# Two convolution modules: the chunk of transform tables moved ahead of the last chunk of input weights, with the second section's transform

## The reference, cut to what matters

```python
def conv_module(h, w_in, b_in, dw_w, dw_b, ln_g, ln_b, w_out):
    a, gt = jnp.split(h @ w_in + b_in, 2, axis=-1)   # (256, 1024) -> two of (256, 1024)
    u = a * jax.nn.sigmoid(gt)
    u = dwconv(u, dw_w, dw_b)                        # depthwise along the tokens, 31 taps
    u = layernorm(u, ln_g, ln_b)
    return jax.nn.silu(u) @ w_out                    # (256, 1024)
```

## Time and profile before

| | us |
|---|---|
| median of three runs | 1610.09 |
| lowest and highest | 1609.86, 1610.27 |
| the profiled execution's own time | 1610.04 |
| span of the profiled execution | 1608.1 |
| TensorE busy in the span | 1573.2 |
| VectorE busy | 1248.2 |
| ScalarE busy | 996.0 |

### The profile page before, as it was taken

How to read it: one execution, slowest core, us unless ns; L and a number is a source line. 1 busy time by engine, 2 the same in 40 slices (tenths; PEclk the granted TensorE clock), 3 DMA queues, 4 the chain that set the end, 5 groups by cost and what they waited for, 6 DMA issues and landing times.

```text
span 1608.1 us, 25361 instructions
## 1 busy us (share of the span) xinstructions
PE 1573.2 (98%) x8810; PEld 1344.2 (84%) x8810; DVE 1248.2 (78%) x1828; ACT 996.0 (62%) x1406; POOL 102.4 (6%) x110
## 2 busy tenths in 40 slices
PE   9999999999999999999999999999999999999998
PEld 9887888878878889868888898868788887878887
DVE  6756888878798887866888886456788887878887
ACT  6576665675676656666666655444666666666664
POOL 0031000000000001340000042000100000000000
PEclk9999999999999999999999999999999999999999
DMA  9434455543645554443555555524555554345553
GB/s 344 153 111 171 181 188 203 183 174 115 239 162 186 195 192 158 165 151 131 183 201 184 189 190 191 195 105 158 183 195 183 185 180 183 140 149 186 185 198 135
DMA packets 43393, 285.44 MB, mean 177 GB/s; under 512 B 5280, under 2 KB 5408, under 8 KB 10688
## 3 DMA queue, kind: packets, MB, share of 16 engines
q1 hardware_dynamic: 40592, 274.96, 47.7%
q0 software_dynamic: 2736, 9.60, 1.8%
HBM read 282.43 MB, written 1.05 MB: 176 GB/s over the span
## 4 chain that ended last, share of the span: by engine, by line
PE 80%; DVE 12%; ACT 5%; issue 3%; DMA 0%; SPq 0%; POOL 0%; DVEq 0%
PE bank L2263 21%; PE bank L2266 10%; PE bank L2162 7%; PE bank L2163 7%; PE bank L2164 7%; PE bank L2112 4%; PE bank L2113 4%; PE bank L2114 4%; DVE w_lo L1230 3%; PE bank L2059 3%; PE bank L2060 3%; PE bank L2061 3%; DVE arena L1527 2%; DVE arena L1513 1%; DVE arena L1510 1%
## 5 line engine op out<-in xcount | busy, mean ns | idle before, releaser
L2263 PE MATMUL bank<-h_both,w_hi 128*128 128x512 f32 x1760 | 554.7, 396 | 10.3 <-DVE arena L1510 6.2
L2266 PEld LDWEIGHTS bank<-h_both,w_lo 128*128 128x128 f32 x1760 | 330.6, 188 | 77.6
L1230 DVE TENSOR_TENSOR w_lo<-raw,w_hi 128x2048 fp32r<-128x2048 f32 (+3 forms) x133 | 289.9, 2180 | 104.3 <-ACT w_hi L698 103.6
L2266 PE MATMUL bank<-h_both,w_lo 128*128 128x256 f32 x1760 | 346.0, 278 | 0.0
L698 ACT ACTIVATE w_hi<-raw 128x2048 fp32r<-128x2048 f32 (+3 forms) x135 | 245.1, 1816 | 100.6 <-PE bank L2164 37.3
L2263 PEld LDWEIGHTS bank<-h_both,w_hi 128*128 128x128 f32 x1760 | 271.6, 189 | 17.6 <-issue 8.2
L1547 DVE TENSOR_TENSOR w_lo<-raw,w_hi 128x2048 fp32r<-128x2048 f32 x120 | 274.1, 2284 | 0.0
L2162 PE MATMUL bank<-w_hi,h_both 128*128 128x512 f32 x632 | 247.9, 392 | 4.2 <-DVE h_both L1541 4.2
L2163 PE MATMUL bank<-w_lo,h_both 128*128 128x512 f32 x632 | 246.2, 390 | 0.0
L2164 PE MATMUL bank<-w_hi,h_both 128*128 128x512 f32 x632 | 246.1, 389 | 0.0
L919 ACT ACTIVATE w_hi<-raw 128x2048 fp32r<-128x2048 f32 x120 | 228.4, 1904 | 0.0
(11 more groups left out here) (236 smaller groups left out, 1858.0 us busy)
## 6 DMA issues: line engine op xcount, KB each, us to landing
raw<-wstream SPq DMA_DIRECT2D x252, 1024.0 KB, 4.8
raw<-wstream SPq DMA_DIRECT2D x8, 256.0 KB, 3.9
raw<-wstream SPq DMA_DIRECT2D x4, 512.0 KB, 8.1
arena<-dilated_bias POOLq DMA_DIRECT2D x8, 256.0 KB, 4.8
arena<-conv_rows POOLq DMA_DIRECT2D x2, 1024.0 KB, 4.7
arena<-window_bias POOLq DMA_DIRECT2D x4, 512.0 KB, 6.0
raw<-wstream SPq DMA_DIRECT2D x4, 384.0 KB, 3.5
cst<-consts SPq DMA_DIRECT2D x1, 1088.0 KB, 11.9
```

The costliest lines, as they stand in the source:

```text
L1230: nc.vector.tensor_tensor(w_lo[:, s, 0:w], raw[:, s, 0:w], w_hi[:, s, 0:w].bitcast(F32), ALU.subtract)\
L2263: nc.tensor.matmul(halves(up_banks(a)[:, m, :]), w[m][0], h_both[:, kt, :, :], start=kt == 0, stop=kt == 7, skip_group_check=True)
L2266: last = nc.tensor.matmul(up_banks(a)[:, m, 0:S], w[m][1], h_hi[:, kt, :], start=False, stop=kt == 7, skip_group_check=True)
```

## The change

The table chunk and the last input chunk change places in the stream: the tables are c8, the last input chunk is c9. On TensorE `transform(1)` stands ahead of `w_in(7)`, and `inverse(0)` is cut into its two token halves, with `transform(2)` between them. On VectorE `wave_parts(0)` goes behind the split of c9, `products(1)` goes ahead of `biased_pair(3, 0)` and `wave_parts(1)` between the two halves of that pair. On ScalarE `wave_parts(1)` goes ahead of the gates of group 3, and the high half of c11 moves from behind `y_evac_conv(0)` to the SiLU loop, behind its second tile. The last input chunk counts on a semaphore of its own (`last_in`), since the tables, which have the lower number, are in use for longer; the end of `inverse(2)` counts both chunks. The third part of section 1 goes to slot 14 of `h_both` in place of slot 4, which `w_in(7)` still reads. The diff, cut to its core:

```diff
-        return [CH] * 5 + [DFT] + [CH] * 3 + [2 * DFT] + [CH] * 4
+        return [CH] * 5 + [DFT] + [CH] * 2 + [2 * DFT] + [CH] * 5
...
+            second = (2, 3, 14)[b]
+            return (slice(8 + 2 * b, 10 + 2 * b), slice(second, second + 1), slice(5 + b, 6 + b))[e]
...
                     def y_evac_conv(e):
                         first, n = section(e)
-                        if e < 2:
-                            act.wait_ge(unwaved, 2 * (k["conv"] - 1) + e + 1)
-                        else:
+                        if e == 1:
+                            act.wait_ge(unwaved, e0 + 3)
+                        elif e == 2:
                             act.wait_ge(first_unwaved, k["conv"])
                         for t in range(1 + (e < 2)):
+                            if e == 0:
+                                act.wait_ge(unwaved, e0 + t + 1)
...
                     split_hi(c0 + 10)
+                    wave_parts(1)
                     gate(3, 0)
                     gate(3, 1)
                     parts(3)
-                    wave_parts(1)
                     y_evac_conv(0)
-                    split_hi(c0 + 11)
                     wave_parts(2)
...
-                        if t == 5:
+                        if t == 1:
+                            split_hi(c0 + 11)
+                        elif t == 5:
                             split_hi(c0 + 12)
...
                     split_lo(c0 + 8)
-                    wave_parts(0)
                     gated_parts(2)
                     split_lo(c0 + 9)
-                    rest_rows(c0 + 9)
+                    wave_parts(0)
+                    rest_rows(c0 + 8)
+                    products(1)
                     biased_pair(3, 0)
+                    wave_parts(1)
                     biased_pair(3, 1)
                     gated_parts(3)
-                    products(1)
-                    wave_parts(1)
                     stats(0, (0,))
                     products(2)
                     wave_parts(2)
...
-                        last.then_inc(unwaved if e < 2 else chunk_used, 1)
+                        if e < 2:
+                            last.then_inc(unwaved, 1)
+                        else:
+                            last.then_inc(chunk_used, 2)
...
-                    w_in(7, 8)
-                    transform(1, c0 + 9)
-                    inverse(0, c0 + 9)
-                    transform(2, c0 + 9)
-                    inverse(1, c0 + 9)
+                    transform(1, c0 + 8)
+                    w_in(7, 9)
+                    inverse(0, c0 + 8, (0,))
+                    transform(2, c0 + 8)
+                    inverse(0, c0 + 8, (1,))
+                    inverse(1, c0 + 8)
                     keep_busy(20, bank[5])
-                    inverse(2, c0 + 9)
+                    inverse(2, c0 + 8)
```

More of the change, by code:

```diff
@@ L307, in build_program @@
         rest_table = sem("rest_table")
+        last_in = sem("last_in")
         unwaved, y_out, y_stats, y_normal = sem("unwaved"), sem("y_out"), sem("y_stats"), sem("y_normal")
@@ L371, in wave_slots @@
         def wave_slots(e, b):
-            return (slice(8 + 2 * b, 10 + 2 * b), slice(2 + b, 3 + b), slice(5 + b, 6 + b))[e]
+            second = (2, 3, 14)[b]
+            return (slice(8 + 2 * b, 10 + 2 * b), slice(second, second + 1), slice(5 + b, 6 + b))[e]
         def glu_slot(g, t):
@@ L1084, in y_evac_conv @@
                         first, n = section(e)
-                        if e < 2:
-                            act.wait_ge(unwaved, 2 * (k["conv"] - 1) + e + 1)
-                        else:
+                        if e == 1:
+                            act.wait_ge(unwaved, e0 + 3)
+                        elif e == 2:
                             act.wait_ge(first_unwaved, k["conv"])
                         for t in range(1 + (e < 2)):
+                            if e == 0:
+                                act.wait_ge(unwaved, e0 + t + 1)
                             ins = nc.scalar.activation(y_conv[:, t, first:first + n], y_bank_conv(e, t)[:, 0:n], ACT.Copy)
-                        ins.then_inc(y_out, 1)
+                            if e == 0:
+                                ins.then_inc(y_out, 1)
+                        if e:
+                            ins.then_inc(y_out, 1)
                     def y_evac_last():
@@ L1726, in biased_pair @@
                             dve.wait_ge(wide_half, k["wide"])
+                        elif g == 3:
+                            dve.wait_ge(last_in, k["conv"])
                         else:
-                            dve.wait_ge(chunk_used, c0 + (1, 3, 6, 8)[g] + 1)
+                            dve.wait_ge(chunk_used, c0 + (1, 3, 6)[g] + 1)
                         if g:
@@ L1798, in stats @@
                         first, n = section(e)
-                        dve.wait_ge(y_out, e0 + e + 1)
                         for t in halves_:
+                            dve.wait_ge(y_out, 4 * (k["conv"] - 1) + (e + 2 if e else t + 1))
                             for at in range(first, first + n, GROUP):
@@ L2097, in feature_chunk, with token_chunk @@
                 last.then_inc(chunk_used, 1)
-            def token_chunk(c, second, h0=0, n_k=4, free=None, wait_h=None, banks=None):
+            def token_chunk(c, second, h0=0, n_k=4, free=None, wait_h=None, banks=None, done=None):
                 pe.wait_ge(lo_done, c + 1)
@@ L2116, in token_chunk @@
                         last.then_inc(wide_half, 1)
-                last.then_inc(chunk_used, 1)
+                last.then_inc(chunk_used if done is None else done, 1)
             def sums(sources, matrix=None, width=S, start=True, stop=True):
@@ L2380, in transform, with inverse @@
                         last.then_inc(waved if e else chunk_used, 1)
-                    def inverse(e, c):
+                    def inverse(e, c, halves_=(0, 1)):
                         _, n = section(e)
@@ L2386, in inverse @@
                         if e == 2:
-                            pe.wait_ge(y_out, e0 + 1)
+                            pe.wait_ge(y_out, 4 * (k["conv"] - 1) + 2)
                         pe.wait_ge(rest_table, k["conv"])
-                        for t in range(2):
+                        for t in halves_:
                             for b in range(2):
@@ L2401, in w_in @@
                         token_chunk(c0 + c, n % 2, free=free, wait_h=k["hlo"] if g == 0 else None,
-                                    banks=(glu_bank(g, 0), glu_bank(g, 1)))
+                                    banks=(glu_bank(g, 0), glu_bank(g, 1)), done=last_in if n == 7 else None)
                     pe.wait_ge(conv_loaded, 112 * k["conv"])
@@ L2691, in pack_weights @@
             ins = [half for flat in pairs for half in (flat[:, :4], flat[:, 4:])]
-            for blocks in (*[[i] for i in ins[:5]], [fwd], *[[i] for i in ins[5:]], [fwd, inv]):
+            for blocks in (*[[i] for i in ins[:5]], [fwd], *[[i] for i in ins[5:7]], [fwd, inv], [ins[7]]):
                 put(*blocks)
```

## The result

The changed kernel took 1615.24 us in the median of 11 runs (1612.68 to 1617.05), the kernel before 1610.4 in 11 runs beside it (1609.86 to 1612.56). The ratio is 1.0026, with a 95% interval of 1.0017 to 1.0036: slower by 4.2 us by the ratio (2.7 to 5.8 us). That is more than the 3.2 us that I called noise, though the lower end of the interval lies within it. The median is 0.2 us above the upper end of the range I gave; the time by the ratio, 1614.3 us, is inside it.

What follows compares the result with a forecast made beforehand. VectorE's backlog was taken as the limit before `inverse(2)`; 1.0 us more in each of two convolutions takes the span from 1608.1 to 1610.1, the execution to 1612.0, the median to 1612.1 us. Range 1609.0 to 1615.0.

Steps and rivals of the forecast that it cites:

- What bounds the kernel: Before `inverse(2)` of each convolution: VectorE's backlog is the limit; at best the 1.13 us TensorE wait goes.
- VectorE's walk: Step-by-step VectorE times from `biased_pair(2, 0)` at 374.70 to group 3's low halves at 391.0 and 391.6.
- The new wait: TensorE, before `transform(2)`: waits 2.2 us for the first low half of group 3, due at 391.0.
- What ends last: Before `inverse(2)`: the 20 transposes end last, so it starts at 398.7 against 397.68, each convolution 1.0 us longer.
- The other edits: c11's high half in the SiLU loop, in time by 0.7 us, and the semaphore, slot and double count: costed at nothing.
- The clock: Rival: TensorE's clock falls behind the wait before `transform(2)`; 1615.9 us with one convolution hit, 1619.7 with both; chance 0.13.
- my bound of 1.5: Upper bound per convolution, if VectorE's two group 3 waits for ScalarE and the first matmul after idling each cost 0.2 more.
- One of my own signs of being wrong: Signs listed: granted clock under 1.00 around 391 us, no wait before `transform(2)`, or a wait before c11's output products.
- The price I set, 3.8 us a fall: `transform(2)` and the second half of `inverse(0)` at half speed: 3.8 us more, between nothing and 7.7 us.
- c11 coming late: Rival: in the SiLU loop c11 is late by up to 1 us in each stage, 1614.1 us; chance 0.04.
- a mild fall of the clock: Allowance in the range's upper part, which reaches to 1615.0 us, for TensorE's clock falling mildly.
- The rival that group 3's low halves would be ready when TensorE asks for them: At 388.8, before `transform(2)`: only TensorE's queue counts, up to 1.3 us gained per convolution, 1607.5 us; chance 0.07.

Runs made afterwards that it cites:

- The experiment with eight transposes: The changed kernel with 8 instead of 20 transposes in front of `inverse(2)`: median 1613.35 us, ratio 1.0017.
- the long execution: Longest of 8 runs of the changed kernel repeated without edit, profiled: 1617.10 us, clock 0.996; the 8 runs had median 1615.74 us, ratio 1.0031.

## Why the prediction was right and wrong

**What bounds the kernel: right.** VectorE's backlog set the start of `inverse(2)` before, and TensorE's own work did not move.

**VectorE's walk: right.** I had group 3's first low half at 391.0 and the second at 391.6; TensorE started at 391.26 and the pair ended at 390.70 + 0.99 = 391.69. The largest step off was 0.12 us, at `biased_pair(3, 1)`, 389.12 for 389.0.

**The new wait: right.** 2.2 us forecast, 2.23 and 2.25 measured, put down to VectorE's low halves.

**What ends last: right in kind, 0.25 us short.** `inverse(2)` was to start at 398.7, 1.0 us late, and started at 398.90. Against a profile that runs 0.03 us early, that is 1.25 us, inside my bound of 1.5. The 0.2 us were in the start of `transform(2)`, which I had at 391.05. Twice 1.25 is 2.5 of the 2.6 us of the span. The split was off: I had 0.7 to 0.8 us for the transposes and 0.3 for VectorE's longer chain. The experiment with eight transposes puts 0.58 us on the transposes, and VectorE's low halves of section 2 end at 398.22 against 397.58 before, 0.64 us later.

**The other edits: right.** c11's high half in the SiLU loop delayed no product, and the new semaphore cost nothing.

**The clock: the step that failed.** One of my own signs of being wrong, a granted clock under 1.00 around 391 us, is in the profile of the long execution, though not in that of the short one. I had the right evidence, a fall after 2.2 us without a matmul at the execution's end, and weighed it down with "the matmuls on both sides are dense", giving it 0.13. By their clock it was what happened in most executions: 13 of 19 had a mean clock of 0.998 or less, against 3 of 29 of the kernel before. The price I set, 3.8 us a fall, was too high: 1.44 and 1.52 us in the long execution and 1.34 and 1.26 in the kernel without transposes. I had priced all of `transform(2)` and the second half of `inverse(0)` at half speed; in conv0 the clock was back at full by 395 us, when `transform(2)` was nearly done, and in conv1 it fell only after `transform(2)` had begun. The two errors worked against each other in the range, but not in the forecast: the likeliest time should have been 1612.1 plus one or two falls of 1.4 us, 1613.5 to 1615. With that, slower by over 0.2% would have been about as likely as not, and I gave it 0.15. That 1614.3 us, the time by the ratio, lies in my range is in part luck: the forecast's own bounds end at 1613.1, and only the room that I had left for c11 coming late and a mild fall of the clock holds it. The reading behind it was also too coarse. I treated the clock as something that either holds or falls for a kernel, when the same program did both from one execution to the next. The rule of the Trainium skill that I cited ("TensorE: Matmul & The Clock Gate", section "HAM oscillation"), half of the throttled time as the price, roughly agrees with the rows here: the fall in the kernel before without transposes cost 1.34 us over a stretch of 3.5 us at a mean clock of 0.53, where half the time at the lower level, by my estimate from that clock, is about 1.6.

**Rivals.** The rival that group 3's low halves would be ready when TensorE asks for them fell at once. That c11 comes late did not happen. The version that gives what the change was after needed one more move, `wave_parts(1)` behind group 3's low halves, and fewer transposes.

## What to carry to other kernels

When an operation is brought forward on a busy engine, list what it pushes back, and give each pushed step the time at which someone asks for it: here 4.4 us of products and low halves went ahead of something that TensorE wanted 1.6 us after the last input chunk, and only the 3.3 us of products were worth having there. Count a long wait of TensorE twice, once as itself and once as a fall of its clock with a price and a chance per execution, and put both into the likeliest time. Filler work that hides an idle stretch becomes the path when the work around it moves, so its length is to be set again after each such change.

## What the runs showed of the hardware that I had not expected

The granted clock fell in some executions of the same program and not in others, and in some places and not in others. After a single wait of 2.2 us between dense matmuls it fell in both convolutions in one profile, in one of two in another, in neither in a third; after 3.3 us it fell in both. Waits of 0.6 to 1.1 us, three in a row, left it at 0.999 or 1.000 in all 8 executions. In two of the three falls behind a wait of 2.2 us the clock went down 1.1 and 1.4 us after the matmuls had gone on, in the third at the end of the wait. Each fall cost 1.3 to 1.5 us. The kernel before has falls too, in 3 to 8 of 29 executions (1611.3 to 1612.4 us, clock 0.998 or 0.999), and one profile of the changed kernel shows such a fall in the stage nat, behind two waits of 0.94 and 0.39 us between short matmuls.
